# Wide moving operand in the two later up products of a two-block transformer kernel

## The reference, cut to what matters

```python
def sq_relu_mlp(h, w_in, w_out):
    return jnp.square(jax.nn.relu(h @ w_in)) @ w_out
# w_in: (2, 1024, 4096), w_out: (2, 4096, 1024)
h = h + sq_relu_mlp(rmsnorm(h, norm_mlp[i]), mlp_w_in[i], mlp_w_out[i])   # i = 0, 1
```

## Time and profile before

| what | value |
|---|---|
| median of three runs | 941.15 us |
| span of the profiled execution | 938.7 us |
| instructions in it | 18179 |
| PE, PE weight loads | 911.1 us (97%), 861.7 us (92%) |
| DVE, ACT | 614.4 us (65%), 496.2 us (53%) |
| DMA | 176.90 MB, mean 188 GB/s |
| mean granted TensorE clock | 0.994 |

### The profile page before, as it was taken

The page is one execution under the profiler, slowest core; times in us unless marked ns, Lnnn a source line. Parts: engine busy times, 40 slices in busy tenths (PEclk is TensorE's granted clock), DMA queues, the critical chain, the costliest instruction groups (busy, mean ns, idle before and its releaser), DMA issues.

```text
span 938.7 us, 18179 instructions
## 1 busy us (share of the span) xinstructions
PE 911.1 (97%) x7609; PEld 861.7 (92%) x7609; DVE 614.4 (65%) x971; ACT 496.2 (53%) x727; POOL 0.2 (0%) x4
## 2 busy tenths in 40 slices
PE   5899999999999999999999999999999999999996
PEld 2688788999999999878999999998999999999996
DVE  1655675776776776887765555576886766666554
ACT  4537674754555567665644343346666654333442
POOL 0000000000000000000000000000000000000000
PEclk9899999999999999999999999999999999999999
DMA  9988757665455568415365555555443655555531
GB/s 351 371 290 282 259 180 256 208 249 205 172 176 211 180 174 177 99 46 156 115 214 195 197 197 196 174 180 179 136 135 102 214 179 181 179 180 184 192 120 45
DMA packets 130701, 176.90 MB, mean 188 GB/s; under 512 B 19696, under 2 KB 108188, under 8 KB 130620
## 3 DMA queue, kind: packets, MB, share of 16 engines
q1 hardware_dynamic: 130140, 174.10, 56.3%
q10 hardware_dynamic: 480, 1.64, 0.5%
HBM read 174.68 MB, written 1.05 MB: 187 GB/s over the span
## 4 chain that ended last, share of the span: by engine, by line
PE 86%; DVE 6%; ACT 4%; DMA 3%; issue 2%; SPq 0%; DVEq 0%; ACTq 0%
PE psum L1569 25%; PE psum L1561 24%; PE psum L1562 24%; DMA raw<-in_w_ada_dram 2%; DVE w_lo L943 2%; PE psum L1663 1%; PE psum L1565 1%; PE psum L1566 1%; ACT w_hi L522 1%; PE psum L2114 1%; PE psum L2048 1%; PE psum L2069 1%; PE psum L2058 1%; DMA raw<-in_w_in_dram 1%; DVE h_lo L978 1%
## 5 line engine op out<-in xcount | busy, mean ns | idle before, releaser
L522 ACT ACTIVATE w_hi<-raw 128x2048 fp32r<-128x2048 f32 (+1 forms) x139 | 264.4, 1904 | 148.0 <-PE psum L1569 120.7
L1561 PE MATMUL psum<-h_hi,w_hi 128*128 128x256 f32 x1352 | 328.9, 283 | 1.5 <-DVE h_lo L1106 1.1
L943 DVE TENSOR_TENSOR w_lo<-raw,w_hi 128x2048 fp32r<-128x2048 f32 (+1 forms) x139 | 313.2, 2277 | 25.6 <-ACT w_hi L522 25.5
L1562 PE MATMUL psum<-h_lo,w_hi 128*128 128x256 f32 x1352 | 324.7, 280 | 0.0
L1561 PEld LDWEIGHTS psum<-h_hi,w_hi 128*128 128x128 f32 x1352 | 253.9, 188 | 9.8 <-issue 7.4
L1562 PEld LDWEIGHTS psum<-h_lo,w_hi 128*128 128x128 f32 x1352 | 255.5, 189 | 0.2
L1569 PE MATMUL psum<-h_hi,w_lo 128*128 128x256 f32 x1352 | 187.0, 280 | 0.6 <-DVE w_lo L943 0.5
L1561 PE MATMUL psum<-a_hi,w_hi 128*128 128x256 f32 x720 | 171.5, 280 | 0.7 <-DVE a_lo L1289 0.5
L1569 PEld LDWEIGHTS psum<-h_hi,w_lo 128*128 128x128 f32 x1352 | 170.1, 188 | 1.5 <-DVE w_lo L943 1.2
L1562 PE MATMUL psum<-a_lo,w_hi 128*128 128x256 f32 x720 | 171.1, 279 | 0.0
L1562 PEld LDWEIGHTS psum<-a_lo,w_hi 128*128 128x128 f32 x720 | 135.8, 189 | 0.0
(11 more groups left out here) (264 smaller groups left out, 766.2 us busy)
## 6 DMA issues: line engine op xcount, KB each, us to landing
raw<-in_mlp_w_in_dram SPq DMA_DIRECT2D x32, 1024.0 KB, 5.5
raw<-in_mlp_w_out_dram SPq DMA_DIRECT2D x32, 1024.0 KB, 7.2
raw<-in_w_ada_dram SPq DMA_DIRECT2D x24, 1024.0 KB, 7.8
raw<-in_w_up_dram SPq DMA_DIRECT2D x22, 1024.0 KB, 5.1
raw<-in_gla_w_in_dram SPq DMA_DIRECT2D x12, 1024.0 KB, 5.2
raw<-in_w_down_dram SPq DMA_DIRECT2D x11, 1024.0 KB, 5.5
raw<-in_w_in_dram SPq DMA_DIRECT2D x10, 1024.0 KB, 7.8
raw<-in_w_out_dram SPq DMA_DIRECT2D x4, 1024.0 KB, 5.8
```

Of the source, the lines that this page charges most:

```text
L522: act.activation(halved(w_hi, m % SPLIT_SLOTS, SPLITS[m]), halved(raw, r % RAW_SLOTS, SPLITS[m]), ACT.Copy).then_inc(*mark("w_hi", m))
L943: dve.tensor_tensor(halved(w_lo, m % SPLIT_SLOTS, key), halved(raw, r % RAW_SLOTS, key), halved(w_hi, m % SPLIT_SLOTS, key).bitcast(F32), ...
L1561: pe.matmul(dst, high, both[0], start=start, stop=False, skip_group_check=True)
L1562: return pe.matmul(dst, high, both[1], start=False, stop=False, skip_group_check=True)
```

## The change

`h_hi` and `h_lo` become the two halves of one tensor, so that the 256 rounded activations and the 256 remainders of one inner block lie side by side. In the two MLP layers one weight load of `w_hi` and one matmul of 512 columns replace the two of 256. The rounded part's product lands in columns 0 to 255 of the bank, the remainder's in 256 to 511; the 8 matmuls on `w_lo` add into the lower half as before. The activation then joins the halves: ACT copies the upper half to `ff_v`, DVE adds the lower half to it, and `max`, `rstd` and the rest work on `ff_v`. The first feed-forward part, attention, the gated mixer and all down products keep two matmuls of 256.

```diff
-        h_hi = sb("h_hi", [P, KT, S], F32R)
-        h_lo = sb("h_lo", [P, KT, S], F32R)
+        h_both = sb("h_both", [P, KT, 2, S], F32R)
+        h_hi, h_lo = h_both[:, :, 0, :], h_both[:, :, 1, :]
...
             def mlp_act(layer, i):                      # ScalarE
                 for f in range(2):
-                    act.wait_ge(*at("dve_read", "mlp_in", layer, i, f))
+                    act.wait_ge(*at("job", "mlp_in", layer, i, f))
+                    if i > 0:
+                        act.wait_ge(*at("mlp_scaled", layer, i - 1, f))
+                    act.activation(ff_v[:, f, :], bank("mlp_in", layer, i, f)[:, S:2 * S], ACT.Copy)\
+                        .then_inc(*mark("mlp_by_low", layer, i, f))
+                for f in range(2):
+                    act.wait_ge(*at("mlp_scaled", layer, i, f))
...
                 for f in range(2):                      # VectorE
-                    dve.wait_ge(*at("job", "mlp_in", layer, i, f))
+                    dve.wait_ge(*at("mlp_by_low", layer, i, f))
+                    dve.tensor_tensor(ff_v[:, f, :], bank("mlp_in", layer, i, f)[:, 0:S], ff_v[:, f, :], ALU.add)\
+                        .then_inc(*mark("dve_read", "mlp_in", layer, i, f))
+                for f in range(2):
+                    dve.wait_ge(*at("dve_read", "mlp_in", layer, i, f))
...
-                    dve.scalar_tensor_tensor(out=ff_g[:, f, :], in0=bank("mlp_in", layer, i, f)[:, 0:S], scalar=0.0,
-                                             in1=rstd[:, :], op0=ALU.max, op1=ALU.mult)\
-                        .then_inc(*mark("dve_read", "mlp_in", layer, i, f))
+                    dve.scalar_tensor_tensor(out=ff_g[:, f, :], in0=ff_v[:, f, :], scalar=0.0, in1=rstd[:, :],
+                                             op0=ALU.max, op1=ALU.mult).then_inc(*mark("mlp_scaled", layer, i, f))
...
+            def high_by_wide(dst, high, k):             # TensorE
+                return pe.matmul(dst[:, :], high, h_both[:, k, :, :].rearrange("p n s -> p (n s)"), start=(k == 0), stop=False,
+                                 skip_group_check=True)
...
+            def wide_tile(idx, key, m, midway=None):
+                slot = weights(key)
+                dst = take(pe, *key, m)
+                for k in range(KT):
+                    operand(idx, k)
+                    high_by_wide(dst, wview(w_hi, slot, KT)[:, k, m * P:m * P + P], k)
+                if midway is not None:
+                    midway()
+                low_weights(key)
+                for k in range(KT):
+                    ins = crossed(dst[:, 0:S], wview(w_lo, slot, KT)[:, k, m * P:m * P + P], h_hi[:, k, :], k == KT - 1)
+                ins.then_inc(*mark("job", *key, m))
```

More of the change, by code:

```diff
@@ L225 @@
             5: ("mlp_in", 0, MLP_STEPS - 1), 6: ("gla", 12), 7: ("gla_out", 3), 8: ("mlp_in", 1, MLP_STEPS - 1)}
-FIRST_USE = {("out", 0), ("gate", 0), ("qkv", 0), ("mlp_in", 0, 0), ("mlp_in", 1, 0)}
+FIRST_USE = {("out", 0), ("gate", 0), ("qkv", 0)}
 USES = {"in": 0, "out": 1, "gate": 2, "val": 2, "qkv": 3, "gla": 6}
@@ L1301, in mlp_act @@
                         dve.wait_ge(*at("rstd", 4 + 2 * layer))
-                    dve.scalar_tensor_tensor(out=ff_g[:, f, :], in0=bank("mlp_in", layer, i, f)[:, 0:S], scalar=0.0,
-                                             in1=rstd[:, :], op0=ALU.max, op1=ALU.mult)\
-                        .then_inc(*mark("dve_read", "mlp_in", layer, i, f))
+                    dve.scalar_tensor_tensor(out=ff_g[:, f, :], in0=ff_v[:, f, :], scalar=0.0, in1=rstd[:, :],
+                                             op0=ALU.max, op1=ALU.mult).then_inc(*mark("mlp_scaled", layer, i, f))
                 for f in range(2):
-                    dve.wait_ge(*at("dve_read", "mlp_in", layer, i, f))
+                    dve.wait_ge(*at("mlp_scaled", layer, i, f))
                     dve.tensor_tensor(ff_s[:, f, :], ff_g[:, f, :], ff_g[:, f, :], ALU.mult)\
@@ L1853, in mlp_up @@
                     ring["set"] = range(4)
+                if i == 0:
+                    key = ("mlp_in", layer, 0)
+                    slot = weights(key)
+                    dst = [take(pe, *key, j) for j in range(2)]
+                    for k in range(KT):
+                        operand(5 + 3 * layer, k)
+                        for j in range(2):
+                            high_by_wide(dst[j], wview(w_hi, slot, KT)[:, k, j * P:j * P + P], k)
+                    low_weights(key)
+                    for j in range(2):
+                        for k in range(KT):
+                            ins = crossed(dst[j][:, 0:S], wview(w_lo, slot, KT)[:, k, j * P:j * P + P], h_hi[:, k, :], k == KT - 1)
+                        ins.then_inc(*mark("job", *key, j))
+                    used(key, ("job", *key, 1))
+                    return
                 if m is None:
-                    project_chunk(5 + 3 * layer, ("mlp_in", layer, i))
+                    project_chunk(5 + 3 * layer, ("mlp_in", layer, i), wide_tile)
                     return
-                feature_tile(5 + 3 * layer, ("mlp_in", layer, i), m,
+                wide_tile(5 + 3 * layer, ("mlp_in", layer, i), m,
                              (lambda: factor(4 + 2 * layer)) if m == 0 else None)
```

## The result

| | before | changed |
|---|---|---|
| median of 20 runs each | 942.12 us | 944.05 us |
| span of the profiled execution | 938.7 us | 941.9 us |

Ratio 1.0024, 95% interval 1.0017 to 1.0032: the change makes the kernel slower by 0.24%, which is clear of the noise of 20 runs each; 934.9 us was forecast.

What follows compares the result with a forecast made beforehand. PE's own pace was taken as the bound: -7.66 us from shorter tiles, +0.96 and +0.43 at the two heads, -6.27 in sum, so 941.15 becomes 934.9 us. Own range 933.5 to 936.5 (60%); 932.7 to 939.5 holds 80%.

Steps and rivals of the forecast that it cites:

- the pace of a wide matmul: MLP tiles: a 512-column float32r matmul takes 216.2 ns, against 233.3 ns for the pair it replaces, 17.1 ns less.
- the term -7.66 us: MLP layers: 448 pairs in 56 tiles, each pair 17.1 ns shorter on PE.
- the fixed cost: Rival, MLP tiles: every matmul has 10 ns besides its stream, a wide one takes 223.3 ns; 938.2 us, 20%.
- the stream is the pace: Rival, MLP tiles: the stream itself takes 280 cycles per 256 columns, so tiles save nothing; 943.0 us, 10%.
- The sign that I gave for the fixed cost: Steady MLP windows: eight 512-column matmuls above 1.79 us show this rival, above 1.85 us the next one.
- Heads: Before each MLP layer's first `down`, the longer activation chain delays PE: +0.96 us in layer 0, +0.43 in layer 1.
- PE's waits: Before the first `down` of each MLP layer, PE idles about 2.0 us in layer 0 and 1.0 in layer 1.
- Covers: Steady MLP steps: slack hides the longer activation chain, 0 us in all 28; tightest 2.0 and 0.29 us left.
- the last `down`: End of each MLP layer: `w_lo` is ready at 5.31 us, wanted at 5.60, so 0 us with 0.29 left.
- Outside the MLP and the layout: Rest of the kernel: outside the MLP layers the trace keeps its length.
- forecast 10.93: Steady MLP windows: a step's distance falls from 11.20 to 10.93 us.

Runs made afterwards that it cites:

- wide_nojoin: Changed kernel without the join: wide matmuls, but the activation reads only the lower half, leaving out the remainders' product; 0.9993 of the kernel before.
- pace: Separate program computing no layer: rows of 64 matmuls of one form, other engines idle; rounded float32r operands take 227.0 ns at 512 columns, 119.8 at 256.
- wide_at_0: Changed kernel with 32 unused bytes ahead of its activations, so they begin at a multiple of 64 bytes; 937.47 us, 0.9958 of the kernel before.
- layout: Kernel before with only the new layout of activations (rounded values and remainders side by side), all matmuls narrow, no join; 0.9998 of the kernel before.
- head_narrow: Kernel before with ACT's rounding and DVE's `w_lo` of the first `down` chunk moved where they don't delay the activation; 1.0009 of the kernel before.
- head_wide_at_0: Changed kernel with 32 unused bytes ahead of the activations, chunk 0's join copies ahead of Ln, rounding and first `down` `w_lo` moved; 0.9985 of before.
- pace_tiles: Separate program repeating the MLP's tiles with no layer computed, other engines idle; a wide tile takes 2.79 us, a tile of pairs 2.88.
- narrow_at_0: Kernel before with 32 unused bytes ahead of its activations, so they begin at a multiple of 64 bytes; 947.38 us, 1.0053 of the unmoved kernel.

## Why the prediction was wrong

**The step that failed is the pace of a wide matmul.** I took 216.2 ns from float32 rows (lines 2114 and 2122) and read the 10 ns that a narrow matmul shows besides its stream as a weight load that hides under a longer one. Measured: 233.3 ns, so the term -7.66 us is 0, as `wide_nojoin` shows without the join. `pace` contradicts the reading too: there 13.1 ns come on top of 256 columns and 13.7 on top of 512, so the longer stream hides nothing, and a quarter of the weight columns takes off only 6.5. That speaks for my first rival, the fixed cost, which would have given 938 us. But in the full kernel the extra is 10.0 ns on 256 columns (116.7), 13.0 on 384 (173.0) and 20.0 on 512 (233.3), where the fixed cost wants 10 each time and the stream 10, 15 and 20; neither reading fits all three. Plain float32 rows were the wrong neighbours although their stream length and weight width were the right ones: at what I read as the same 512 cycles the float32 instruction takes 216.2 ns and the float32r matmul of 512 columns 226.7 to 237.7 in the programs here. Why the two types differ is not shown.

**The rival "the stream is the pace" came true in its numbers**, at this placement: step 11.20 us, eight wide in 1.87 us, 943.0 us forecast for it, and 1.0024 x 941.15 = 943.4 measured. I gave it 10% because rows of another type seemed to speak for less. The row could not separate stream and load, as I wrote; that called for a chance nearer to the forecast's. Its mechanism, a stream of 280 cycles per 256 columns, is not shown: `pace` has 227.0 ns where it wants 233, and `wide_at_0` 228.9. The sign that I gave for the fixed cost, above 1.79 us for eight, was that reading's own value (8 x 223.3 ns) and should have stood below it; the measured 1.87 us is above either mark.

**Heads.** Layer 0: +0.96 forecast, +0.83 by the trace. The chain from Exp to `a_lo` grew by 0.87; the two copies overlap (0.64 for both). Layer 1: 0.84 in that rival, 0.74 measured. PE's waits, 2.0 and 1.0 us in the forecast, are 1.36 and 0.56. That is close to 1.45 and 0.59, the forecast less the 0.55 and 0.41 us by which the tiles did not become shorter.

**Covers.** No step has a PE wait inside, and the wait on `w_lo` is 0.6 us in two, where it was 0.5. DVE starts the next `w_lo` 3.0 us behind `down`, as worked out. Zero was right, also for the last `down`.

**Outside the MLP and the layout:** 0, as `layout` shows.

**Not seen at all** was that the pace depends on where operands lie. With 32 bytes of padding the step comes out as forecast (10.95 us, forecast 10.93), but that is luck: two thirds of what it saves is in untouched matmuls, by a cause that I didn't name.

**Still open** is what decides the beat, and with it why a wide matmul takes just the time of two narrow ones here. Shown is that 32 bytes of place change the median by -0.7% (changed kernel), +0.5% (kernel before) and, in the changed kernel, +0.6% and +0.2% when `h_both`, or `a_hi` and `a_lo` with all behind `h_both`, move by 32 bytes without the other, with every instruction the same. Shown as well is that the beat changes at one place: in `head_narrow` between two layers of one execution, and from `wide_at_0` to `head_wide_at_0`. Neither a rule of 64 bytes nor one by operand holds. Other positions of `w_hi` and `w_lo` in the full kernel were not tried, nor was the start of the MLP shifted in time with all else the same.

## What to carry to other kernels

Merging two matmuls into one with the same number of columns leaves the stream as long as it was, so it can save only what the second matmul costs besides its stream (10 ns here, of which nothing was saved). Measure this per type at the kernel's own placement before counting on it, and don't borrow it from another type's row. Where PE is the bound and the gain hoped for is a per cent, compare both versions at two placements of their operands: here 32 bytes turned +0.24% into -0.45% of the unmoved kernel before, and into -1.0% of the one moved likewise. A join that hides in every steady step still shows where a layer's first activation is awaited; put the part that needs no `rstd` ahead of it.

## What the runs showed of the hardware

- Float32r matmuls ran between 113.3 and 125 ns at 256 columns and between 226.7 and 237.7 ns at 512, at the full clock (granted clock 1.00), by place and program. In the steady MLP the starts repeat: 116, 117, 120, 114 ns in the kernel before (four take 466.7); 113, 113, 114 in `wide_at_0` (three take 340).
- With 32 or 64 weight columns in `pace` the pace of 256 columns was 113.3 and 113.4 ns, where 128 weight columns took 119.8. Full weights ran at 113.3 as well in `wide_at_0`, and at 512 columns 64 weight columns took 229.8 ns against 227.0.
- Bf16 matmuls, each with its weight load, held 8 in 1.73 us at 512 columns (`pace_tiles`) and 64 in 6.99 us at 256 (`pace`), 216.2 and 109.2 ns. The Trainium skill (TensorE: Matmul & The Clock Gate, Back-to-back issue gap) gives 215.8 and 109.2 by its N/2.4 + 2.5, and these rows agree; its other figure, about 131 ns a matmul sustained at N=512, is shown by no run here. For float32r N/2.4 + 2.5 is 4 to 22 ns short.
- The same 32 bytes also changed the first block's feed-forward part, where all matmuls are narrow: the window from 200 to 300 us started 860 matmuls in the kernel before and 859 in the changed one, but 851 in `narrow_at_0` and 852 in `wide_at_0`, all at a granted clock of 1.00.
